# A hybrid S5 / attention / expert layer: parameter loads on ScalarE's queue, x loaded and turned in two halves, and one load group of the final sum split

## The reference

```python
a = rmsnorm(h, g_mix)                 # h = x, (1, 512, 1024)
z = a @ w_in                          # w_in (1024, 2048): u_ssm | q | k | v
y_ssm = rmsnorm(s5_mixer(z[..., :512], a_re, a_im, log_dt, b_re, b_im, c_re, c_im, d_skip, w_glu), g_ssm_out)
y_att = diff_attention(...)           # 4 heads, two causal softmax maps each, rotary
h = h + concat(y_ssm, y_att) @ w_out
h = h + cross_attention(rmsnorm(h, g_x), rmsnorm(mem, g_mem), wq_x, wk_x, wv_x, wo_x)
h = h + moe(rmsnorm(h, g_ffn), ...)   # 64 SwiGLU experts, 8 for each token, and a shared one
return rmsnorm(h, g_final)
```

## Time and profile before

| | |
|---|---|
| Time, median of 3 runs | 1204.99 us (1203.58 to 1205.38) |
| The profiled execution | 1200.21 us, of which the span is 1198.4 us |
| Mean granted TensorE clock | 0.958 of full speed |
| PE busy | 1085.9 us, 91% |
| DVE, ACT, POOL busy | 400.0, 221.0, 148.3 us |
| Chain that ended last | PE 80%, DVE 7%, DMA 6%, ACT 4% |

### The profile page before, as it was taken

The page is one execution under the profiler, slowest core; times in us unless marked ns, Lnnn a source line. Parts: engine busy times, 40 slices in busy tenths (PEclk is TensorE's granted clock), DMA queues, the critical chain, the costliest instruction groups (busy, mean ns, idle before and its releaser), DMA issues.

```text
span 1198.4 us, 13248 instructions
## 1 busy us (share of the span) xinstructions
PE 1085.9 (91%) x5027; PEld 524.1 (44%) x5027; DVE 400.0 (33%) x922; ACT 221.0 (18%) x479; POOL 148.3 (12%) x194
## 2 busy tenths in 40 slices
PE   5999798987799987999899999999899998999955
PEld 3444486754444454444344433333234334443312
DVE  1784564353202012106931212122122222212166
ACT  3221422335202023003101111111111111111102
POOL 3000004220000000000022121212112121121110
PEclk9999899888899998999899999999899999999977
DMA  6225313221126240222579999999999999999994
GB/s 206 71 71 130 77 54 98 71 70 71 36 70 281 71 175 1 69 70 106 219 276 416 422 420 420 420 422 420 420 420 421 420 420 422 420 421 417 415 411 195
DMA packets 76960, 300.55 MB, mean 251 GB/s; under 512 B 20853, under 2 KB 24218, under 8 KB 50266
## 3 DMA queue, kind: packets, MB, share of 16 engines
q1 hardware_dynamic: 64218, 265.01, 56.4%
q0 software_dynamic: 12672, 34.62, 7.3%
HBM read 282.03 MB, written 27.53 MB: 258 GB/s over the span
## 4 chain that ended last, share of the span: by engine, by line
PE 80%; DVE 7%; DMA 6%; ACT 4%; issue 2%; SPq 1%; DVEq 0%; POOL 0%; POOLq 0%
PE ps L768 26%; PE ps L1159 24%; PE ps L1175 12%; PE ps L1141 3%; DMA act_t<-in_w_down 3%; PE ps L891 2%; PE ps L904 2%; DMA z<-expert_rows 2%; PE ps L1245 2%; PE ps L1043 1%; PE ps L1019 1%; PE ps L1183 1%; PE ps L749 1%; DVE z L2009 1%; DVE z L1836 1%
## 5 line engine op out<-in xcount | busy, mean ns | idle before, releaser
L1159 PE MATMUL ps<-ring,z 128*32 128x512 f32 (+2 forms) x1056 | 285.1, 597 | 1.1 <-DVE z L2063 1.0
L768 PE MATMUL ps<-dw,act_t 128*128 128x512 f32 x576 | 250.7, 596 | 4.0 <-issue 3.1
L768 PEld LDWEIGHTS ps<-dw,act_t 128*128 128x128 f32 x576 | 109.4, 191 | 141.1 <-issue 139.9
L1175 PE MATMUL ps<-ring,act_t 128*32 128x512 f32 (+2 forms) x528 | 146.6, 599 | 1.2 <-DVE act_t L2080 0.8
L1159 PEld LDWEIGHTS ps<-ring,z 128*32 128x32 f32 (+2 forms) x1056 | 90.6, 131 | 110.9 <-issue 108.7
L1159 PE MATMUL ps<-dw,z 128*64 128x512 f32 (+2 forms) x256 | 98.9, 594 | 0.9 <-issue 0.6
L1159 PE MATMUL ps<-z 128*32 128x512 f32 (+2 forms) x288 | 87.2, 621 | 4.5 <-issue 4.5
L1508 ACT ACTIVATE tok<-ps 128x256 f32<-128x256 f32 x44 | 16.9, 385 | 306.2 <-PE ps L1159 306.2
L2038 DVE COPY z<-ps 128x512 f32<-128x512 f32 x44 | 30.4, 692 | 113.4 <-PE ps L1175 113.4
L1175 PEld LDWEIGHTS ps<-ring,act_t 128*32 128x32 f32 (+2 forms) x528 | 43.8, 131 | 49.6 <-issue 47.0
L2202 POOL COPY ixb<-tabs 128x1 uint32<-128x1 uint32 x88 | 17.4, 198 | 381.3 <-DVE z L2038 366.1
(11 more groups left out here) (315 smaller groups left out, 1227.9 us busy)
## 6 DMA issues: line engine op xcount, KB each, us to landing
ring<-in_w_gate SPq DMA_DIRECT2D x42, 1024.0 KB, 23.6
ring<-in_w_up SPq DMA_DIRECT2D x42, 1024.0 KB, 28.8
ring<-in_w_down SPq DMA_DIRECT2D x42, 1024.0 KB, 29.2
dw<-in_w_gate SPq DMA_DIRECT2D x11, 1024.0 KB
dw<-in_w_up SPq DMA_DIRECT2D x11, 1024.0 KB
act_t<-in_w_down SPq DMA_DIRECT2D x11, 1024.0 KB
z<-in_w_gate SPq DMA_DIRECT2D x11, 1024.0 KB, 24.0
z<-in_w_up SPq DMA_DIRECT2D x11, 1024.0 KB, 28.2
```

What stands on the lines that cost most here:

```text
L768: ins = pe.matmul(ps[0:m, bank0 + j, 0:n], lhs(w, q * 4 + c4, c4, j), rhs(w, q * 4 + c4, c4, j), start=(q == 0 and c4 == 0), stop=(q == le ...
L1159: ins = pe.matmul(ps[rows, 2 + r % 2, :], xtt[r % 2][:, c, rows], ring_wgu(BUF[x])[:, :, c, :], start=(c == 0), stop=(c == NC_D - 1))
L1175: ins = pe.matmul(ps[rows, 5 + n, :], htt[r % 2][:, c, rows], ring_wd(BUF[x])[:, c, n * 512:(n + 1) * 512], start=(c == 0), stop=(c == 1))
```

## The change

Four edits. First, SP now issues `cst`, then x in two loads of 1 MB, each with 512 of the columns of all four tiles, then w_in. Each half has its own semaphore (`s_x[0]`, which counts the constants too, and `s_x[1]`). Second, the nine small loads stand at the start of ACT's list, `log_dt` first. Third, PE turns chunks 0 to 3 of x first, then the parameter rows, then chunks 4 to 7; the first half of the first product waits for the copies of four chunks only (`s_tea`, `s_tev` at 2) and the second for all. ACT's squares and roots now stand behind its copies of the turned x, and DVE's `rstd` behind its own. Fourth, in the table of the tail the loads (1, 0) and (1, 1) have one semaphore and (1, 2) and (1, 3) another. Three pairs of semaphores are merged into one each with higher counts (`s_rx` and `s_rm` into `s_dev`, `s_pc` and `s_bc` into `s_pc`; the constants moved from `s_prow` to `s_x[0]`).

```diff
     @block.sync
-        sp.dma_start(cst[:], consts[:, 0:NCONST]).then_inc(s_prow, 16)
-        for i in range(NT):
-            sp.dma_start(h[:, i, :], t["x"][0, i * P:(i + 1) * P, :]).then_inc(s_x, 16)
-        for r, name, n in ((R_ARE, "a_re", 16), (R_AIM, "a_im", 16)):
...
-        sp.dma_start(st[0:16, 90:92], t["log_dt"].rearrange("l (a k) -> (l k) a", a=2),
-                     allow_slow_non_contiguous=True).then_inc(s_ldt, 16)
+        sp.dma_start(cst[:], consts[:, 0:NCONST]).then_inc(s_x[0], 16)
+        for hf in range(2):
+            cols = slice(hf * 512, (hf + 1) * 512)
+            sp.dma_start(h[:, :, cols], t["x"][0].rearrange("(i p) d -> p i d", p=P)[:, :, cols]).then_inc(s_x[hf], 16)
...
-    LOADED = [[0, 0, 1, 1], [2, 2, 2, 2], [3, 3, 4, 4], [5, 6, 7, 8]]
+    LOADED = [[0, 0, 1, 1], [2, 2, 3, 3], [4, 4, 5, 5], [6, 7, 8, 9]]
...
     @block.scalar
-        squares(0, NT, h, tok3, D, [[(s_x, 16 * NT)]] + [[]] * 3)
-        roots(1, slice(0, NT), slice(8, 8 + NT))
+        act.dma_start(st[0:16, 90:92], t["log_dt"].rearrange("l (a k) -> (l k) a", a=2),
+                      allow_slow_non_contiguous=True).then_inc(s_ldt, 16)
+        for r, name, n in ((R_ARE, "a_re", 16), (R_AIM, "a_im", 16)):
+            act.dma_start(prow[r:r + n, :].rearrange("k (a p) -> k a p", a=2),
+                          t[name][0].rearrange("(a k) p -> k a p", a=2)).then_inc(s_prow, 16)
+        for r, name, n in ((R_GMIX, "g_mix", 8), (R_GX, "g_x", 8), (R_GMEM, "g_mem", 8), (R_GFFN, "g_ffn", 8),
+                           (R_GSSM, "g_ssm_out", 4), (R_GSUB, "g_sub", 1)):
+            act.dma_start(prow[r:r + n, :], t[name].rearrange("l (c p) -> (l c) p", p=P)).then_inc(s_prow, 16)
         act.wait_ge(s_pc, 1)
         link(act.activation(pcol[:], ps[:, 7, 0:NROWS], ACT.Copy))
         act.activation(gcat[:, 0:4], pcol[:, R_GSSM:R_GSSM + 4], ACT.Copy).then_inc(s_pce, 1)
         turned(0, pcol[:, R_GMIX:R_GMIX + 8], S, at3)
+        squares(0, NT, h, tok3, D, [[(s_x[0], 32), (s_x[1], 16)]] + [[]] * 3)
+        roots(1, slice(0, NT), slice(8, 8 + NT))
...
     @block.vector
+        dve.wait_ge(s_pce, 1)
+        turned(0, pcol[:, R_GMIX:R_GMIX + 8], S, at3)
         dve.wait_ge(s_sq, NT)
         rstd(1, st[:, 0:NT], D, st[:, 8:8 + NT], rs_x)
-        dve.sem_inc(s_rx, 1)
-        dve.wait_ge(s_pce, 1)
-        turned(0, pcol[:, R_GMIX:R_GMIX + 8], S, at3)
+        dve.sem_inc(s_dev, 1)
```

More of the change, by code:

```diff
@@ L448, in hybrid_layer @@
     s_rows = sem("all_rows_scattered")
-    s_yl = [sem(f"rows_loaded{i}") for i in range(9)]
+    s_yl = [sem(f"rows_loaded{i}") for i in range(10)]
     s_red = sem("tile_rows_summed")
@@ L507, in hybrid_layer @@
     gf = z[:, 0:D]
-    LOADED = [[0, 0, 1, 1], [2, 2, 2, 2], [3, 3, 4, 4], [5, 6, 7, 8]]
-    OF_LOAD = [sum(row.count(n) for row in LOADED) for n in range(9)]
+    LOADED = [[0, 0, 1, 1], [2, 2, 3, 3], [4, 4, 5, 5], [6, 7, 8, 9]]
+    OF_LOAD = [sum(row.count(n) for row in LOADED) for n in range(10)]
     sq_junk = view(act_t, 0, NT, D)
@@ L716, in _ @@
             sp.wait_ge(e_gu, NR)
-            for n in range(3):
+            for n in range(4):
                 sp.wait_ge(s_yl[n], 16 * OF_LOAD[n])
@@ L742, in _, with turn @@
     def _(pe):
-        def turn(done, n_tok, src, waits):
-            for c in range(NC_D):
+        def turn(done, n_tok, src, waits, chunks=range(NC_D)):
+            for c in chunks:
                 for i in range(n_tok):
@@ L782, in weight_rhs, with second_half_turned @@
             return w4(w)[:, c4, :]
-        pe.wait_ge(s_prow, 16 * 9)
+        turn(s_tf, NT, h, lambda c, i: [(s_x[0], 32)] if c == i == 0 else [], chunks=range(4))
+        pe.wait_ge(s_prow, 16 * 8)
         pe.wait_ge(s_ldtw, 1)
         pe.transpose(ps[:, 7, 0:NROWS], prow[0:NROWS, :], ident[0:NROWS, 0:NROWS]).then_inc(s_pc, 1)
-        turn(s_tf, NT, h, lambda c, i: [(s_x, 16 * NT)] if c == i == 0 else [(s_pce, 1)] if c == 7 and i == 0 else [])
-        pe.wait_ge(s_tea, 4)
-        pe.wait_ge(s_tev, 4)
+        turn(s_tf, NT, h, lambda c, i: [(s_x[1], 16)] if c == 4 and i == 0 else [(s_pce, 1)] if c == 7 and i == 0 else [],
+             chunks=range(4, NC_D))
+        pe.wait_ge(s_tea, 2)
+        pe.wait_ge(s_tev, 2)
+        def second_half_turned():
+            pe.wait_ge(s_tea, 4)
+            pe.wait_ge(s_tev, 4)
         for cb in range(4):
```

26 lines of the change are left out of this document (10 added, 16 removed).

## The result

| | before | after |
|---|---|---|
| Median of 4 runs each, in one comparison | 1204.28 us (1202.40 to 1205.38) | 1193.30 us (1187.20 to 1195.93) |
| Ratio after to before | | 0.9909, 95% interval 0.9888 to 0.9930 |
| The profiled execution | 1200.21 us, span 1198.4 | 1195.93 us, span 1194.1 |
| Mean granted TensorE clock | 0.958 | 0.957 |

The changed kernel is faster, by more than I forecast. The two profiled executions are only 4.3 us apart, the medians 11.0; after's profiled execution is the slowest of its four. Most of what follows is about that difference.

The account below looks back on a forecast made before the run. The prediction took loads and the order of ACT's and DVE's lists to bound the head, PE what follows. Head 6.2 plus tail 2.1 made 8.3 us, from 1204.99 to 1196.7 us; range 1194 to 1201.5.

Parts of the forecast that it names:

- What bounds the kernel, and direction: Whole kernel: loads and the order of ACT's and DVE's lists bind before 19.34 us, PE behind it; the change is faster.
- The head, 6.2 us: Before the first product: its start moves from 19.34 to 13.1 us, gaining 6.2 us, worst 3.6, best 6.6.
- The place of the new start: Head: first product starts at 13.1 us, after copies of four chunks, x's second half turned and w_in's first block.
- Parameter rows at 9.0 and hidden: Head: small loads on ACT's queue land at 9.0 us, hidden by x's first sixteen transposes until 10.4.
- b_re's 14.9: Head, rival of late parameter rows: last lands at 14.9 us, head gives 2.1, total 1200.8 us; chance 0.13.
- What is late next: Behind the product's start: second half, squares, root and lambda loads stay hidden; DVE about 1.7 us late against PE, costing nothing.
- my 9 to 10: End of the first product: DVE's wait for PE before its memset falls from 11.29 us to 9 to 10.
- All of it slides: From 129.9 us on: waits are released by PE, DVE or ACT in one chain, so the head's gain carries through.
- The tail, 2.1 us: Final sum: PE starts q = 1 early, is then bound by loads; gains 2.1 us, between 0 and 2.5.
- the split does nothing: Final sum, rival: PE starts sooner but ends with the loads, only the head is left, 1198.8 us; chance 0.12.
- The slower rival, the clock in the tail: Final sum: gaps on PE hold the clock at 1.2 GHz, sum +5.9 us, so 1210.9; chance 0.04.
- From the sum to the time: Whole kernel: 8.3 us gained, taken from the median of 1204.99 us, gives 1196.7 us.

Follow-up runs that it names:

- e2: The whole change but with the old table of the tail, so the head alone: median 1194.60 us, ratio 0.9936 to the kernel before.
- e11: The kernel before, unchanged, run once more with a profile: 1200.22 us.
- e3b: The kernel before with the new table of the tail and s_rx and s_rm merged to free a semaphore: median 1200.12 us, ratio 0.9983.
- e4: The kernel before with merged semaphores alone (s_rx with s_rm, s_bc with s_pc): median 1202.89 us, ratio 0.9991.
- e12: The kernel before with fourteen spare transposes filling PE's idle time ahead of the first product: median 1202.08 us, ratio 0.9989.
- e10: The kernel before with small loads on ACT's queue and copies ahead of squares and rstd, x in whole tiles, old tail: median 1202.42 us, ratio 1.0011.
- e14: A repeat: the kernel before with small loads on ACT's queue and squares behind the copies, x in whole tiles, old table: median 1202.75 us, ratio 1.0008.
- e5: The kernel before with only the nine small loads moved to the start of ACT's list: median 1203.78 us, ratio 1.0019.
- e9: The whole change with g_final's load issued behind the last four row loads instead of ahead of them: median 1193.69 us, ratio 0.9925 to the kernel before.
- e17: The whole change, unchanged, run again in a third session: median 1195.73 us, ratio 0.9952 to the kernel before.

## Why the prediction was right and wrong, point by point

**What bounds the kernel, and direction: right.** The head is bound by loads and by the order of ACT's and DVE's lists, and PE behind it carries an earlier start through the first product without a loss (110.56 us before and after).

**The head, 6.2 us: too small.** This is the step of the sum that failed. The mechanism came as written, its size did not: e2 measured 8.25 us by the medians, 7.7 by the ratio. The place of the new start was right. I had 13.1, and the five profiles with the whole new head have 12.11, 12.73, 12.79, 13.25 and 13.42. Wrong was what I subtracted it from. I took 19.34 from the one profile of before, and the other profiles with the old head start later, at 19.70 (e11), 19.95 (e3b) and 20.52 (e4), with x landing later. By the means of these profiles the start moved 7.0 us, from 19.9 to 12.9. The 7.2 us of the first pair of profiles is an early one of each: the first half of x landed at 6.37 in after, and PE began to turn it at 6.73 to 7.63 in the other four, around the 7.0 that I had. And a term was not in the sum. PE's idle time before the product disappears, and with it the fall of the clock behind it: about 1 us (e12: 0.8 to 1.3). I had looked for the clock in the tail only, and took its 1.00 at the head from one execution. Start and clock make 7.8 to 8.3, which agrees with e2.

**Parameter rows at 9.0 and hidden: right.** They had landed when PE came to them, at 9.79, and log_dt took 2.3 us where it took 4.5. Where PE waits for the rows, with x in whole tiles, the last came at 8.60 (e10), 9.75 (e14) and 9.79 (e5). So 9.0 was a fair estimate, b_re's 14.9 was not, and the cover until 10.4 is thin.

**What is late next: right.** Second half, squares, root and lambda loads are all hidden. But DVE's path was not as I had it. The lambda loads landed at 30.99 instead of 30.08, and DVE began on `craw`'s copies at 45.12 instead of 48.62, without a wait. That is 3.5 us sooner where PE was 7.2 sooner, so DVE was 3.7 us late against PE, not 1.7. It made this up later: its next work behind ACT's squares began at 103.94 instead of 112.04. So the wait of 12.15 us came out above my 9 to 10.

**"All of it slides": wrong as a forecast of one execution.** I found no event bound to clock time and was right on the waits, but the attention stage varies from 158 to 170 us under the same code. In the profiled pair it swallowed all 7.2 us. The range had no term for it. It may also take a part of the gain in the medians: 7.0 for the start, about 1 for the clock and 2 to 3 for the tail are 10 to 11 us, and over all runs the change is 9.0 us faster. Three of the five profiles with the whole new head have the long form, none of the four with the old one. Whether the change makes it more frequent is not shown.

**The tail, 2.1 us: right.** e3b gives 2.0 to 3.0. From the end of the last expert's product to the end of the chain it is 48.24 us in before and 46.40 in after, and over nine profiles of each table (without e9) the medians are 48.24 and 46.67; but the single ones overlap, 46.6 to 48.9 and 45.1 to 47.6. The first rows on PE, the wait of 0.62 us and a tail bound by loads came as written. The rival "the split does nothing" is refuted by the same run.

**The slower rival, the clock in the tail: refuted.** The early records ran at 0.50 and 0.61 until 1157, as forecast, but from there the clock stayed at 1.00 through gaps of 1.28 us and less.

**From the sum to the time: too high a base.** I subtracted 8.3 from 1204.99, the median of three runs. The median of 137 is 1202.84. Both errors pull the same way, towards too long a time: over all runs the base was 2.2 us too high and the gain, 9.0, 0.7 us more than I had; in the comparison of record it was 0.7 us of base and 2.7 of gain. The range's low end, 1194.0, was the forecast's own best head and tail with the spread of three runs, and after's own runs spread over 15 us. That the time fell just outside is in part luck: e17's twelve runs of the same kernel have a median of 1195.73, inside the range. The short head is no luck, as e2 shows. A small slip in the chances: 0.04 and half of 0.04 make 0.06 for slower, not 0.05.

## What to carry to other kernels

When several lists of instructions meet at one start, price the edits together: queue and order alone did not move the start, and both together moved it by 2 to 4 us (e10, e14). Then measure the time too, for those two showed no gain in it. A gap on PE that an edit removes is worth its length and, in some executions, the slow clock behind it, so look at the granted clock there in more than one execution. And before a small gain is read from two profiles, compare the stages that the change doesn't touch; here one of them differed by as much as the head had won.

## What the runs showed of the hardware

The same instructions after the same gap of 2.72 us ran at a granted clock of 0.59 in one execution and 1.00 in another, so that sixteen records took 6.42 or 3.72 us. In all 19 profiles the slow form of this block goes with the long form of a stage in which PE and DVE wait for each other, 164.4 to 169.9 us instead of 158.3 to 162.0. That the slow block makes the stage long is likely, and not shown. Behind the idle time before the first product, 2.24 to 2.65 us left the clock at 1.00 in three profiles, and 2.98 us was followed by 0.50 in two; that the length decides it is not shown. The same page and section of the Trainium skill puts the cost of such a ramp below 1% of a typical kernel. The 11.7 us by which the stage differs are just below 1% of this one, and above the change's 9.0.
